# State-space loop of a two-block network: Toeplitz blocks through DRAM, the direct term inside the kernel matrix, operands two rounds ahead

## The reference, cut to what matters

```python
# x: 512 positions x 1024 channels. Two attention blocks, then
#   ffn0, s5, ffn1, ffn2, conv, ffn3, each with an RMS norm before and after. The change is in s5.
def s5_mixer(h, w_in, a_re, a_im, log_dt, b_re, b_im, c_re, c_im, d_skip, w_glu, b_glu, w_out):
    u = (h @ w_in).reshape(bsz, seq, 64, 16)              # 64 groups of 16 channels
    abar = exp(dt * (a_re + i a_im))                      # 64 complex states per group
    bb = (abar - 1) / a * b
    bu = einsum('blgh,gph->blgp', u, bb)
    st[l] = abar * st[l-1] + bu[l]                        # along the 512 positions
    y = Re(einsum('blgp,ghp->blgh', st, c)) + d_skip * u
    y = gelu(y)
    z = y * sigmoid(y @ w_glu + b_glu)
    return z @ w_out
```

## Time and profile before

| | us |
|---|---|
| median of 3 runs | 2957.59 |
| lowest, highest | 2954.29, 2957.65 |
| profiled execution, its own time | 2959.4 |
| its span | 2957.6 |
| PE busy over the span | 2776.1 |
| DVE, ACT, POOL busy | 1504.0, 1116.9, 570.6 |
| mean granted clock of PE | 0.953 of 2.4 GHz |

### The profile page before, as it was taken

How to read it: one execution, slowest core, us unless ns; L and a number is a source line. 1 busy time by engine, 2 the same in 40 slices (tenths; PEclk the granted TensorE clock), 3 DMA queues, 4 the chain that set the end, 5 groups by cost and what they waited for, 6 DMA issues and landing times.

```text
span 2957.6 us, 36175 instructions
## 1 busy us (share of the span) xinstructions
PE 2776.1 (94%) x13846; PEld 2280.9 (77%) x13846; DVE 1504.0 (51%) x2120; ACT 1116.9 (38%) x1824; POOL 570.6 (19%) x502
## 2 busy tenths in 40 slices
PE   6999999999999999999689999988999997999998
PEld 5766688766788888888578888876888885888887
DVE  4478445575465442656345443276442584544423
ACT  3248633376443422312333222252222468432222
POOL 1020421113267700234110000047000200200000
PEclk9998989989899999987799999999999999999999
DMA  4220013200133423432222323336323342133232
GB/s 134 100 71 1 15 59 106 80 29 1 43 89 129 135 86 89 129 93 72 71 72 86 99 88 85 97 104 245 99 77 98 129 168 77 58 99 99 80 95 68
DMA packets 295853, 263.09 MB, mean 89 GB/s; under 512 B 44067, under 2 KB 286444, under 8 KB 292140
## 3 DMA queue, kind: packets, MB, share of 16 engines
q1 hardware_dynamic: 290908, 233.65, 25.7%
q0 software_dynamic: 2800, 20.25, 1.7%
q10 hardware_dynamic: 2016, 7.46, 0.8%
HBM read 234.98 MB, written 26.35 MB: 88 GB/s over the span
## 4 chain that ended last, share of the span: by engine, by line
PE 78%; DVE 7%; ACT 5%; issue 4%; DVEq 2%; POOLq 2%; POOL 1%; SPq 0%; DMA 0%; ACTq 0%
PE bank L390 23%; PE bank L392 23%; PE bank L391 22%; PE bank L1843 3%; DVE WL L376 2%; PE bank L1831 2%; ACT WH L371 2%; PE bank L1802 1%; DVE stats L2167 1%; DVEq L2184 1%; PE bank L1239 1%; POOLq L2622 1%; POOLq L2620 1%; PE bank L1803 1%; PE bank L1804 1%
## 5 line engine op out<-in xcount | busy, mean ns | idle before, releaser
L390 PE MATMUL bank<-XH,WH 128*128 128x512 f32 (+1 forms) x2496 | 940.6, 377 | 76.7 <-DVE WL L376 37.0
L392 PE MATMUL bank<-XH,WL 128*128 128x512 f32 (+1 forms) x2496 | 929.3, 372 | 0.0
L391 PE MATMUL bank<-XL,WH 128*128 128x512 f32 (+1 forms) x2496 | 923.9, 370 | 0.0
L376 DVE TENSOR_TENSOR WL<-raw,WH 128x2048 fp32r<-128x2048 f32 (+1 forms) x212 | 453.4, 2139 | 572.7 <-ACT WH L371 572.3
L390 PEld LDWEIGHTS bank<-XH,WH 128*128 128x128 f32 x2496 | 482.2, 193 | 171.7 <-DVE WL L376 36.5
L371 ACT ACTIVATE WH<-raw 128x2048 fp32r<-128x2048 f32 (+1 forms) x212 | 370.0, 1746 | 541.2 <-PE bank L392 541.2
L391 PEld LDWEIGHTS bank<-XL,WH 128*128 128x128 f32 x2496 | 482.6, 193 | 89.4 <-issue 3.3
L392 PEld LDWEIGHTS bank<-XH,WL 128*128 128x128 f32 x2496 | 481.2, 193 | 84.7
L392 PE MATMUL bank<-HH,WL 128*128 128x512 f32 (+1 forms) x792 | 294.4, 372 | 0.0
L390 PE MATMUL bank<-HH,WH 128*128 128x512 f32 (+1 forms) x792 | 293.0, 370 | 0.0
L391 PE MATMUL bank<-HL,WH 128*128 128x512 f32 (+1 forms) x792 | 292.0, 369 | 0.0
(11 more groups left out here) (398 smaller groups left out, 3545.0 us busy)
## 6 DMA issues: line engine op xcount, KB each, us to landing
raw<-in_ffn_w_dram SPq DMA_DIRECT2D x88, 1024.0 KB, 5.3
raw<-in_ffn_w_dram SPq DMA_DIRECT2D x64, 704.0 KB, 4.5
raw<-in_w_in_dram SPq DMA_DIRECT2D x24, 1024.0 KB, 5.1
MM<-mm_scr SPq DMA_DIRECT2D x12, 1152.0 KB, 7.4
raw<-in_w_out_dram SPq DMA_DIRECT2D x8, 1024.0 KB, 5.0
raw<-in_cv_w_in_dram SPq DMA_DIRECT2D x8, 1024.0 KB, 5.5
mm_scr<-MBA POOLq DMA_DIRECT2D x6, 1152.0 KB, 4.4
mm_scr<-MBB POOLq DMA_DIRECT2D x6, 1152.0 KB, 4.7
```

The lines of the kernel that those rows point to most:

```text
L376: dve.tensor_tensor(WL[:, slot, 0:n * P], raw[:, slot, 0:n * P], WH[:, slot, 0:n * P].bitcast(F32), ALU.subtract).then_inc(l_done, 1)
L390: pe.matmul(out, WH[:, slot, c:c + P], h, start=start, stop=False)
L391: pe.matmul(out, WH[:, slot, c:c + P], l, start=False, stop=False)
L392: return pe.matmul(out, WL[:, slot, c:c + P], h, start=False, stop=stop)
```

## The change

- **Toeplitz blocks by transfers.** The response `KS` goes to a DRAM scratch `k_scr` whose first 112 rows (the lags below zero) were zeroed once. `MT` is loaded from it with an overlapping pattern: partition p takes rows p, p+16, ..., 1024 pieces of 512 bytes. `toeplitz` on PE and the copies `kernel_copy` on ACT are gone. In the new `MT` the group is the innermost index, so a block is read with a step of 8 elements, 32 bytes.
- **Direct term.** d on a diagonal, `SD`, made by ACT, is added by one 128-column matmul to the response of lag zero. `skip` on DVE, which added d times u to `YR`, is gone. The powers are kept in descending order, so that u rows are in ascending order and the u tile is one DVE operation that reads PSUM with a step of 32 bytes, where it was one and eight copies.
- **Two rounds ahead.** `MT` and `G1` have two places. PE's round k is swap(k), to_rows(k+2), inputs(k+1), outputs(k). DVE makes `Wt` one round earlier. `CSW(k+2)` is asked for on SP, between the writes of `YS(k)` and the load of `U(k+2)`, and `MT(k+2)` behind that.
- **Gate.** The blocks' halves 4 and 5 are made in rounds 4 to 6, the loads of the last two are moved into rounds 6 and 7, and PE starts the gate with tiles 0 to 6 while tile 7 goes through DRAM. The product's halves go to new tiles `ZH`, `ZL`, pair by pair.

```diff
         def s5_sp(sp, s):
...
+            def cs_load(k):
+                sp.wait_ge(ss(s, f"cs_out{k % 2}"), 16 * (KD // 2))
+                sp.dma_start(CSW[:, k % 2], cs_scr[k]).then_inc(ss(s, f"scr_in{k % 2}"), 16)
...
+            def kernel_load(k):
+                sp.wait_ge(ss(s, "k_out"), at(s, "k_out", 16 * (k + 1)))
+                lags = bass.AP(k_scr.tensor, k_scr[k % 2].offset, [[P, P], [GCH * P, CL], [1, P]])
+                sp.dma_start(MT[:, k % 2], lags).then_inc(ss(s, f"mt{k % 2}"), 16)
...
                 if k + 2 < KD:
+                    sp.wait_ge(ss(s, "x"), at(s, "x", k + 1))
+                    cs_load(k + 2)
+                    sp.wait_ge(ss(s, "ydone"), at(s, "ydone", k + 1))
                     sp.wait_ge(ss(s, "u_in"), at(s, "u_in", 16 * (k + 2)))
                     u_load(k + 2)
+                    kernel_load(k + 2)
...
         def s5_pe(pe, s):
...
+                pe.matmul(bank[6][:, 0:P], SD[:, :], ident[:, :], start=True, stop=False)
                 for g in range(GS):
+                    w = Wt[:, g].rearrange("p s h -> p (s h)")
+                    pe.transpose(bank[4 + g // 4][:, g % 4 * P:(g % 4 + 1) * P], w, ident[:, :])
+                    mm = pe.matmul(bank[6][:, g * GCH:(g + 1) * GCH], w, C1[:, k * GS + g, :], start=False,
+                                   stop=g == GS - 1)
...
-            to_rows(0)
-            toeplitz(0)
-            pe.wait_ge(acc_read, j0 + 8)
-            inputs(0)
-            for k in range(KD):
-                if k + 1 < KD:
-                    to_rows(k + 1)
+            to_rows(0)
+            pe.wait_ge(acc_read, j0 + 8)
+            inputs(0)
+            to_rows(1)
+            for k in range(KD):
                 pe.wait_ge(ss(s, "z"), at(s, "z", k + 1))
                 pe.matmul(bank[2][:, :], s5c[:, S5_SWAP:S5_SWAP + P], work2[:, 0, :], start=True, stop=True)\
                   .then_inc(ss(s, "zswap"), 1)
+                if k + 2 < KD:
+                    to_rows(k + 2)
                 if k + 1 < KD:
-                    toeplitz(k + 1)
                     inputs(k + 1)
...
+                outputs(k)
+            glu(0, range(7))
...
+            glu(1, range(4))
+            glu(0, range(7, KD))
+            glu(1, range(4, KD))
...
         def s5_dve(dve, s):
...
                 dve.tensor_tensor_scan(work2[:, 0, :], flat(RR[:, :, :]), work1[:, 0, :], 0.0, ALU.mult, ALU.add)\
                    .then_inc(ss(s, "z"), 1)
+                if k == 0:
+                    matrices(2)
...
-                if k + 2 < KD:
-                    matrices(k + 2)
-                if k >= 2:
-                    skip(k - 2)
                 if k >= 3:
                     low_y(k - 3)
+                if k + 3 < KD:
+                    matrices(k + 3)
+                if k in (5, 6):
+                    split_l(dve, b0 + k - 1, k - 5, 16)
```

More of the change, by code:

```diff
@@ L62 @@
 S5_JC = CL + 1
[L63 to L64 removed]
+S5_ROWS = S5_JC + NC + 1
+S5_SGN = S5_ROWS + GCH
 S5_SWAP = S5_SGN + 3
 S5_COLS = S5_SWAP + P
+LAGS = (2 * CL - 1) * GCH
 def shape_tables():
@@ L2240, in attn_dve @@
             out_dve(dve, s, b0 + 14, j0 + 28, s0 + 28, YA, post)
-        c_rows = [x[:, :, :, :].rearrange("p g s h -> p g (s h)") for x in (G1, MT)]
+        c_rows = [G1[:, i].rearrange("p g s h -> p g (s h)") for i in range(2)]
         def u_rows(k):
@@ L2291, in s5_sp @@
                     load_block(sp, b0 + 4 + i, i, raw3(i, KD), w[1][:, :, i * 256:(i + 1) * 256])
+            for i in range(2):
+                sp.wait_ge(ss(s, f"mt{i}"), 16)
+            kernel_load(0)
+            kernel_load(1)
             for k in range(KD):
@@ L2362, in inputs, with outputs @@
                 mm.then_inc(ss(s, "s"), 1)
-            to_rows(0)
-            toeplitz(0)
-            pe.wait_ge(acc_read, j0 + 8)
-            inputs(0)
-            for k in range(KD):
-                if k + 1 < KD:
-                    to_rows(k + 1)
-                pe.wait_ge(ss(s, "z"), at(s, "z", k + 1))
-                pe.matmul(bank[2][:, :], s5c[:, S5_SWAP:S5_SWAP + P], work2[:, 0, :], start=True, stop=True)\
-                  .then_inc(ss(s, "zswap"), 1)
-                if k + 1 < KD:
-                    toeplitz(k + 1)
-                    inputs(k + 1)
-                pe.wait_ge(ss(s, "mt"), at(s, "mt", k + 1))
+            def outputs(k):
+                pe.wait_ge(ss(s, f"mt{k % 2}"), 16 * (k // 2 + 2))
                 pe.wait_ge(ss(s, "g1"), at(s, "g1", k + 1))
@@ L2434, in gelu @@
                 act.activation(XH[:, k, :], UN[:, k, :], ACT.Copy).then_inc(ss(s, "gh"), 1)
+            skip(0)
+            kernel_out(0)
+            skip(1)
             rows(0)
-            kernel_copy(0)
+            kernel_out(1)
+            skip(2)
+            rows(1)
             for k in range(KD):
-                if k + 1 < KD:
-                    rows(k + 1)
+                if k + 2 < KD:
+                    kernel_out(k + 2)
+                    if k + 3 < KD:
+                        skip(k + 3)
+                if k in (4, 5):
+                    split_h(act, b0 + k, k - 4, 16, s0 + 6 + 2 * (k - 4))
+                if k >= 2:
+                    gelu(k - 2)
+                if k + 2 < KD:
+                    rows(k + 2)
                 act.wait_ge(ss(s, "ydone"), at(s, "ydone", k + 1))
@@ L2463, in s5_act @@
                 split_h(act, b0 + 6 + i, i % 2, 16, s0 + 10 + 2 * i)
-            for k in range(KD):
-                act.wait_ge(ss(s, "zz"), at(s, "zz", k + 1))
-                act.activation(XH[:, k, :], UN[:, k, :], ACT.Copy).then_inc(ss(s, "h2"), 1)
+                for o in (2 * i, 2 * i + 1):
+                    act.wait_ge(ss(s, "zz"), at(s, "zz", o + 1))
+                    act.activation(ZH[:, o, :], UN[:, o, :], ACT.Copy).then_inc(ss(s, "h2"), 1)
             out_act(act, s, b0 + 8, j0 + 16, s0 + 16, Y5)
@@ L2635, in s5_pool @@
             outmat(0)
-            for k in range(1, KD):
-                decay(k)
-                outmat(k)
+            outmat(1)
+            for k in range(KD - 1):
+                decay(k + 1)
+                if k + 2 < KD:
+                    outmat(k + 2)
             out_pool(pool, s)
```

179 lines of the change are left out of this document (87 added, 92 removed).

## The result

The changed kernel takes 2978.05 us (median; 2965.08 to 2982.24), the kernel before, timed beside it, 2957.62. The ratio is 1.0074, with a 95% interval of 1.005 to 1.0098: slower by 20.4 us. The forecast was 2979.4.

A forecast was written before the change was run, and what follows sets the result against it. PE, busy for 94% of the span, was taken as the bound; +28.3 + 15.6 - 5.3 - 15.3 + 1.5 - 5 + 2 = +21.8 us on 2959.4, less 1.8 for the median, gave 2979.4 us, range 2961 to 2996.

The forecast's parts named there:

- six rounds, with the strided weights: Loop from first to seventh YS: rounds of 22.9 us instead of 18.19, +28.3 us, plus +2 for strided weights.
- first round: Up to the first YS: PE idles behind the response and waits for Wt(2); +15.6 us, give or take 3.
- last round: After the seventh YS: only swap, the way to x and outputs remain, 10.75 us instead of 16.0; -5.3 us.
- gate, to the last sigmoid: Gate: the 15.36 us wait before it goes, -15.3 us; the third block comes late, +1.5.
- output projection: Before the output projection: the wait falls from 5.60 to 1.4 us and PE avoids a low-clock start; -5 us.
- The ring: Loop: inputs(k+1) waits for U(k+1), landing 9.1 us after YS (lower bound 7.75); PE waits 2.1 us a round.
- The clock: Loop: without the dense Toeplitz work PE's granted clock is near 0.5 instead of 0.76; PE alone takes 2.6 us more a round.
- The rule read from the earlier trace: PE in the loop: 64-column matmuls keep a full clock but do not bring it back.
- The strided weights: Matmuls reading MT with a 32-byte step: mostly covered at the low clock, +2 us, bounds 0 and 15.
- Rival 1: The full clock returns and stays, in to_rows and inputs of each round: sum -33 us, 2925 us; 9%.
- Rival 2: U never stops PE in the loop, since the transfers interleave: rounds of 21 us, 2968 us; 17%.
- Rival 4: The clock comes back in some rounds, when swap and SD meet favourably: 20 us less or more, 2957 us; 8%.

The follow-up runs named there:

- e2: Changed kernel with the CSW load put back on ScalarE's queue, right behind YS, U left on SyncE's queue: 2959.1 us, ratio 1.0013.
- e5: Kernel before with its Toeplitz matmuls cut from 128 columns to 16 from the second round on (not a whole kernel): 3013.4 us, ratio 1.0198.
- e1: Changed kernel with the load of U two rounds ahead moved in front of the row writes on SyncE's queue: 2947.8 us, ratio 0.9970.
- e3: Changed kernel with 8 unused dense 128-column matmuls added before the wait for U in each round that has a next one: 2967.1 us, ratio 1.0042.
- e4: Changed kernel with both edits, U first on SyncE's queue and 8 dense matmuls before the inputs: 2950.4 us, ratio 0.9991.
- e7: e1 plus unused dense matmuls spread among to_rows' matmuls, and 8 before and 8 behind to_rows in the first round: 2930.3 us, ratio 0.9923.
- e9: e7 plus ScalarE copying MT so that each group's weights lie side by side, and outputs reading that copy: 2930.7 us, ratio 0.9920.

## Why the prediction was right

The order of the argument held: the loop gets worse through `U` and the low clock, the gate gets better, the first wins. In the profiled execution, by the intervals given above:

| step | forecast | measured | from |
|---|---|---|---|
| six rounds, with the strided weights | +30.3 | +31.7 | 140.77 - 109.11 |
| first round | +15.6 | +13.5 | 1301.70 + 11.83 - 1300.04 |
| last round | -5.3 | -4.6 | 11.44 - 16.05 |
| gate, to the last sigmoid | -13.8 | -15.6 | 46.98 - 62.53 = -15.55 |
| output projection | -5 | -5.7 | (54.16 - 75.37) + 15.55 |
| sum | +21.8 | +19.3 | medians: +20.4 |

**The ring.** `U` lands 9.0 us after `YS` (forecast 9.1), with `CSW` ahead on its queue (e2). The wait is 4.3 us on average, not 2.1. `to_rows` took 4.4 us, not 4.9; its 16-column matmuls are now interleaved with transposes, which may be why, but no run tests it. In some rounds a short stretch at the full clock let PE arrive sooner, and the sixth round has no `to_rows`, where I had priced six equal rounds. As the ring decides, none of this moves the round: 23.46 us measured, 22.9 forecast.

**The clock.** 0.54 in the loop, and e5 shows that the Toeplitz matmuls had held it up. The rule read from the earlier trace rows has two halves. That 64-column matmuls don't bring the clock back fits the profiled e1 (0.50 in all its rounds). That they keep it did not hold for `outputs` with strided weights: in e3, e4 and e7 the clock fell inside `outputs` with no gap on PE, and in e9, with the weights side by side, it held. One phrase was too strong: that nothing is left to restore the clock. In the first three rounds of the changed kernel it came back inside `to_rows` and was gone again before `inputs`. The second of them, where the duration of two 16-column instructions shows the clock:

```profile
1328.36 0.45 PE L2362 MATMUL bank<-C,Wt 128*128 128x16 f32 x2
...
1328.82 0.29 PE L2362 MATMUL bank<-C,Wt 128*128 128x16 f32 x2
...
1334.53 7.09 PE L2374 MATMUL bank<-U,W 128*128 128x64 f32 x32 [4.27 <-DMA U<-u_scr]
```

The clock fell at about 1332.1 (0.91 from 1328.40 to 1330.26, 1.00 from there to 1332.10, 0.51 behind), in the middle of the wait for `U`. So in these rounds the full clock did end in the pause, as the prediction had it. How much more a kernel without the pause would have had from it stays open: the profiled e1 never had the full clock to lose.

**The first round** came 2.1 us sooner than forecast. `to_rows` is 0.5 us shorter each time, and `Wt(2)` was ready 2 us sooner; PE still waited for it, 3.47 us. From the first `to_rows` to the first `YS` PE is busy for 34.55 us with 177 instructions at a clock of 0.58, where it was 25.38 us with 178 at 0.81; it is idle for 5.3 us more, and starts 1.0 sooner. These make the +13.5.

**The strided weights** cost 0.03 us a pair, 8 pairs a round: 2 us in all, as forecast. That was right for this clock only. At the full clock it is 0.25 us a pair, 2 us a round, 16 in all: above the upper bound of 14.7 that I took from ACT's strided read. (That read is gelu's and the plain one a copy's, so their difference wasn't the stride's alone.) Rival 1 (2925 us, the full clock comes back) had 3.6 us for `outputs` in it and would by this have been some 16 us slower than written.

**The rivals.** Rival 1 didn't come: the full clock returned for short stretches and stayed in none. Rival 2 (`U` never stops PE, 21 us a round) is e1: 20.4 in five rounds and 17.0 in the sixth, which I had priced as a full one. Its total, 2968 us, is 20 us above e1's 2947.8; the rounds of the profiled execution explain 7 of these, the rest isn't traced. Rival 4 is seen in small: the three stretches moved nothing, as `U` decided. What I didn't see is that the gate part alone was worth -22 and could be had without the loop's part.

What stays open: how much of the 9.2 us of longer busy time in the first round is clock and how much the other mix of matmuls, for which no run was made; and why e3's burst, and the matmuls behind the pause in e9, brought the clock back in some rounds only.

## What to carry to other kernels

Before matmuls are taken out of a loop, look at what the granted clock did behind them: work that PE does beside a transfer may be what keeps its clock, and its removal can cost more than the work did (e5: less work, 59 us more). When a long chain moves to DRAM, read the queue of the load that becomes critical: its place in the queue was worth 3.6 us a round (e1), though `U` had its two places all along. And a change of two parts should be timed in its parts: one was worth -22 us, which leaves about +42 for the other.
